# A hybrid retention and latent-attention layer on one core: the feed-forward products in a block form with seven products for eight

## The chip, the cores and the metric

The kernel is one program for one core of a Trainium2 chip. It is written in Bass: each engine has its own instruction list, and lists meet only through semaphores that the program names. The metric is the device time of one execution in microseconds (us), lower is better.

## The reference

One layer for 1024 prompt frames and 64 sample frames (1088 columns in all), model width 1024, feed-forward width 2816, everything in float32:

```python
xn = rms_norm(x, norm_mix_w)
rq, rk, rv, rg, cq, ckv, kpe, ga, gb = split_columns(xn @ w_in)
...
ret_y, mla_y, new_state = mixer_core(rq, rk, rv, q, ckv, kpe, w_ukv)
ret_branch = (head_group_norm(ret_y, ret_gn_w).astype(x.dtype) * jax.nn.silu(rg)) @ w_ret_o
mla_branch = mla_y @ w_mla_o
merged = jax.nn.sigmoid(ga) * ret_branch + jax.nn.sigmoid(gb) * mla_branch
h = x + merged @ w_out
g, u = jnp.split(rms_norm(h, norm_ffn_w) @ w_gate_up, 2, axis=-1)
h = h + (jax.nn.silu(g) * u) @ w_down
```

The final RMS norm of h is the output y. The change lies in the last two lines, the feed-forward stage.

## The kernel before

Activations lie feature-major: 128 features on the partitions, a tile for each 128 features, 1088 token columns. Each product is made of three matmuls in a reduced-precision float32 form, so that the sum has nearly float32's precision (`product`, L542 to L546): a number is split into a high part (a copy that rounds, on ScalarE) and a low part (number minus high part, on VectorE or GpSimd), and high x high, low x high and high x low are accumulated in PSUM. Weights and activations are both split.

Weights come as items: one item is the 8 blocks of 128x128 for one output tile, 512 KB. SyncE loads item n into one of two staging buffers, ScalarE writes `w_hi` (`split_high`, L848 to L855), VectorE writes `w_lo` (`split_low`, L1164 to L1169), TensorE runs the item in three column groups of 384, 384 and 320 (`item_units`, L555): 8 x 3 matmuls for each group. Six PSUM banks serve two items in turn.

The stages before the change's place are the input projection, latent attention, retention, the gated merges (two loops of items) and the output projection (`I_OUT`, 8 items), whose evacuation on VectorE (L1505) adds x and leaves h in `res`, while ScalarE squares it and VectorE sums the squares. TensorE adds these over the partitions with a matmul against ones (`feature_sums`, L583 to L591), ScalarE takes the root (`roots`, L873), VectorE the reciprocal (`inverses`, L1193), and then VectorE multiplies each tile of h by gain and reciprocal (L1207), ScalarE writes `xn_hi` (L1116), and VectorE and GpSimd take turns at `xn_lo` (L1180, L1577). TensorE's first item follows tile by tile (`streamed_item`).

The feed-forward stage (TensorE L822 to L843) goes over three groups of hidden tiles, `FFN_GROUPS` = (0, 8), (8, 8), (16, 6). For each hidden tile of a group one gate item and one up item run over the 8 tiles of xn; ScalarE applies Silu to the gate banks, VectorE multiplies with the up banks (L1534), ScalarE and VectorE split the result into `y_hi` and `y_lo`. After a group's up tiles come 8 down items over that group's tiles, and VectorE adds each to `res` (L1552). In the last group ScalarE also squares the result (L1102) and VectorE sums it (L1494) for the final norm, which ends the kernel: sums, roots, reciprocals, eight multiplies, eight stores.

All engine lists are in order: an instruction that waits holds up everything behind it on its engine.

Of the kernel before, what the change touches and what calls it, by code (L numbers as in the profile page):

```python
# [11 lines left out]
P = 128  # L28
# [17 lines left out]
FFN_GROUPS = ((0, 8), (8, 8), (16, 6))  # L46
# [97 lines left out]
def build(nc, a, o):  # L144

    with ExitStack() as ctx:
# [92 lines left out]
        res_sq = region("res_sq", 22, [TOK])  # L239
        res_inv = region("res_inv", 23, [TOK])  # L240
        norm_f = [region(f"norm_f{b}", 18 + b, [TOK]) for b in range(2)]
# [7 lines left out]
        yr_spill = nc.dram_tensor("yr_spill", (8, P, TOK), F32, kind="Internal").ap()  # L249

# [69 lines left out]
        out_done = sem("out_done")  # L320

# [50 lines left out]
        F_OUT, F_FFN, A_FFN = F_M2 + 24, F_M2 + 48, A_M2 + 24  # L372
        SUM_OUT, SUM_FIN = KT + 6, KT + 6 + 24
# [26 lines left out]
        def _(sp):  # L400
# [118 lines left out]
            with sp.Fori(0, 4) as i:  # L519
                for j in range(2):  # L520
                    for g, (c0, c1) in enumerate(GROUPS):
                        k = 3 * j + g
                        sp.wait_ge(g_free, 6 * i + (F_OUT + k - 1))
                        sp.dma_start(tmp[k % 2][:, 0:c1 - c0], a["x"][:, 2 * i + j, c0:c1])\
                          .then_inc(xres_in[k % 2], 16)
                    item_in_loop(i, I_OUT + 2 + j)
            with sp.Fori(0, (N_ITEMS - I_FFN) // 2 - 1) as i:
                for j in range(2):
                    item_in_loop(i, I_FFN + 2 + j)

            for t in range(KT):
                sp.wait_ge(scaled, 2 * KT + 6 + t + 1)
                sp.dma_start(o["y"][:, t, :], res[:, t, :]).then_inc(out_done, 16)
# [7 lines left out]
        def _(pe):  # L541
            def product(out, wh, wl, xh, xl, start=True, stop=True):  # L542

                nc.tensor.matmul(out, wh, xh, start=start, stop=False)  # L544
                nc.tensor.matmul(out, wl, xh, start=False, stop=False)  # L545
                return nc.tensor.matmul(out, wh, xl, start=False, stop=stop)  # L546
# [37 lines left out]
            def feature_sums(k, src):  # L584

                for g, (c0, c1) in enumerate(GROUPS):
                    m = 3 * k + g
                    if m >= 2:
                        pe.wait_ge(root_done, m - 1)
                    nc.tensor.matmul(ps[:, 6 + m % 2, 0:c1 - c0], ones[:, :], src[:, c0:c1],  # L590
                                     start=True, stop=True).then_inc(stat_done, 1)  # L591
# [3 lines left out]
            feature_sums(0, sumsq)  # L595
            streamed_item(I_A % 2, I_A, 0, None, xa_hi, xa_lo, lambda k: wait_low(pe, k))

            def kv_sums():
                pe.wait_ge(summed, KT + 6)
                feature_sums(2, sumsq)  # L600

            for j in range(1, N_A):
# [4 lines left out]
                if j == 4:  # L607
                    pe.wait_ge(summed, KT + 4)
                    feature_sums(1, sumsq)
# [213 lines left out]
            feature_sums(3, res_sq)  # L823
            n0, free0, act0, low0 = I_FFN, F_FFN, A_FFN, 24
            for f, (_, tiles) in enumerate(FFN_GROUPS):
                pe.wait_ge(g_free, free0 - 3)
                if f == 0:

                    streamed_item(n0 % 2, n0, 0, (g_act, act0 - 2), xn_hi, xn_lo,
                                  lambda k: wait_low(pe, KT + 4 + k))  # L830
                    item_units((n0 + 1) % 2, n0 + 1, 3, (g_free, free0 - 2), xn_hi, xn_lo)
                with pe.Fori(1 if f == 0 else 0, tiles) as i:
                    item_units(n0 % 2, 2 * i + n0, 0, (g_act, 3 * i + (act0 - 2)), xn_hi, xn_lo)
                    item_units((n0 + 1) % 2, 2 * i + (n0 + 1), 3, (g_free, 3 * i + (free0 - 2)), xn_hi, xn_lo)
                n0, free0, act0, low0 = n0 + 2 * tiles, free0 + 3 * tiles, act0 + 3 * tiles, low0 + 3 * tiles
                pe.wait_ge(g_low, low0)
                with pe.Fori(0, 4) as i:
                    for j in range(2):
                        item_units((n0 + j) % 2, 2 * i + (n0 + j), 3 * j,
                                   (g_free, 6 * i + (free0 + 3 * j - 5)), y_hi, y_lo, blocks=tiles)  # L840
                n0, free0 = n0 + 8, free0 + 24
            pe.wait_ge(summed, SUM_FIN + 24)
            feature_sums(4, res_sq)  # L843
# [3 lines left out]
        def _(act):  # L847
# [25 lines left out]
            def roots(k, width):  # L873
                for g, (c0, c1) in enumerate(GROUPS):
# [231 lines left out]
            with act.Fori(0, 4) as i:  # L1106
                for j in range(2):
                    for g, (c0, c1) in enumerate(GROUPS):
                        if g == 0:
                            act.wait_ge(g_done, 6 * i + (G_OUT + 3 * j + 1))  # L1110
                            in_loop(i, I_OUT + 1 + j)
                        residual_squares(i, j, g, c0, c1, F_OUT, SUM_OUT)
            roots(3, D_MODEL)
            for t in range(KT):
                act.wait_ge(scaled, KT + 6 + t + 1)
                nc.scalar.activation(xn_hi[:, t, :], norm_f[t % 2][:, :], ACT.Copy).then_inc(norm_high, 1)  # L1116
# [646 lines left out]
```

## Time and profile before

| what | value |
|---|---|
| time, median of 3 runs | 2310.66 us (2310.51 to 2312.24) |
| span of the profiled execution | 2308.3 us |
| TensorE matmul busy | 2131.0 us (92%) |
| VectorE, ScalarE, GpSimd busy | 912.8, 577.7, 117.4 us |
| mean granted TensorE clock | 0.963 of full |
| instructions | 32790 |

The span is the time from the first to the last instruction of the profiled execution; the time of a run is a little longer. Busy time is summed over an engine's instructions. A matmul's shown duration is longer than its distance from the next one, since matmuls overlap: to price one, read the distance between starts. The granted clock is in tenths of the full 2.4 GHz; 0.5 is the lower of its two levels, 1.2 GHz.

### The profile page before, as it was taken

To read this page: it belongs to the slowest core of one execution; us is meant where nothing else is said; L and a number is where in the kernel's file an instruction comes from. 1 tells how busy PE (TensorE), PEld (TensorE's weight loads), DVE (VectorE), ACT (ScalarE), POOL (GpSimd) and SP (SyncE) were. 2 spreads that over 40 slices of the span, in tenths; PEclk is the share of its full clock that TensorE was granted. 3 is DMA by queue.
4 is the path that set the end of the run, shared out by engine and by line. 5 is a ranking of instruction groups with operands and counts; after the bars stand their busy time and mean duration, and the time that the engine had idled before them with its cause. 6 is when DMAs were issued, how large, how long until landed. Compare 5 with 4: busy or idle time off the path is not lost.

```text
span 2308.3 us, 32790 instructions
## 1 busy us (share of the span) xinstructions
PE 2131.0 (92%) x12842; PEld 2046.4 (89%) x12842; DVE 912.8 (40%) x1620; ACT 577.7 (25%) x1069; POOL 117.4 (5%) x145
## 2 busy tenths in 40 slices
PE   3979898997989889999999999699999999999996
PEld 3957787886989879999999999699999999999995
DVE  7476767764434433311112243622222222222245
ACT  4234444441121233311211122222210211112222
POOL 2010000001112210000000000100000000000000
PEclk8989999998999999999999999799999999999998
DMA  6211111115111113211141113111111111111112
GB/s 273 63 52 33 45 44 34 39 34 216 44 45 47 57 34 89 81 46 45 45 191 45 45 46 92 40 46 45 45 46 37 46 45 45 46 44 40 44 55 86
DMA packets 62782, 144.06 MB, mean 62 GB/s; under 512 B 9713, under 2 KB 34225, under 8 KB 62705
## 3 DMA queue, kind: packets, MB, share of 16 engines
q1 hardware_dynamic: 62704, 143.00, 19.1%
q8 instruction: 52, 0.85, 0.1%
q14 instruction: 26, 0.20, 0.0%
HBM read 113.80 MB, written 29.18 MB: 62 GB/s over the span
## 4 chain that ended last, share of the span: by engine, by line
PE 79%; DVE 13%; ACT 3%; DMA 2%; issue 1%; SPq 1%; POOL 1%; DVEq 0%; ACTq 0%
PE ps L544 25%; PE ps L546 25%; PE ps L545 25%; DVE tmp L1215 1%; DVE pt_lo L1180 1%; DVE negmax L1382 1%; DVE inv L1198 1%; DVE w_lo L1168 1%; PE ps L779 1%; DMA y_lo<-ym_spill 1%; PE ps L720 1%; DVE p_exp L1390 1%; DVE norm_f L1207 1%; DMA xn_lo<-xn_spill 1%; PE ps L783 1%
## 5 line engine op out<-in xcount | busy, mean ns | idle before, releaser
L544 PE MATMUL ps<-xn_hi,w_hi 128*128 128x384 f32 (+1 forms) x2016 | 669.0, 332 | 37.7 <-DMA xn_lo<-xn_spill 12.4
L546 PE MATMUL ps<-xn_lo,w_hi 128*128 128x384 f32 (+1 forms) x2016 | 664.9, 330 | 0.0
L545 PE MATMUL ps<-xn_hi,w_lo 128*128 128x384 f32 (+1 forms) x2016 | 664.9, 330 | 0.0
L544 PEld LDWEIGHTS ps<-xn_hi,w_hi 128*128 128x128 f32 x2016 | 384.5, 191 | 44.9 <-issue 19.4
L545 PEld LDWEIGHTS ps<-xn_hi,w_lo 128*128 128x128 f32 x2016 | 384.8, 191 | 0.0
L546 PEld LDWEIGHTS ps<-xn_lo,w_hi 128*128 128x128 f32 x2016 | 384.5, 191 | 0.0
L544 PE MATMUL ps<-y_hi,w_hi 128*128 128x384 f32 (+1 forms) x912 | 299.3, 328 | 9.8 <-DVE y_lo L1180 6.3
L546 PE MATMUL ps<-y_lo,w_hi 128*128 128x384 f32 (+1 forms) x912 | 299.2, 328 | 0.0
L545 PE MATMUL ps<-y_hi,w_lo 128*128 128x384 f32 (+1 forms) x912 | 298.8, 328 | 0.0
L1168 DVE TENSOR_TENSOR w_lo<-w_stage,w_hi 128x1024 fp32r<-128x1024 f32 (+1 forms) x151 | 182.0, 1205 | 240.8 <-ACT w_hi L854 240.4
L854 ACT ACTIVATE w_hi<-w_stage 128x1024 fp32r<-128x1024 f32 (+1 forms) x151 | 156.3, 1035 | 448.0 <-PE ps L546 440.1
L544 PEld LDWEIGHTS ps<-y_hi,w_hi 128*128 128x128 f32 x912 | 172.4, 189 | 11.2 <-issue 7.1
L545 PEld LDWEIGHTS ps<-y_hi,w_lo 128*128 128x128 f32 x912 | 172.4, 189 | 0.0
L546 PEld LDWEIGHTS ps<-y_lo,w_hi 128*128 128x128 f32 x912 | 172.3, 189 | 0.0
L1534 DVE TENSOR_TENSOR tmp<-ps,tmp 128x384 f32<-128x384 f32 (+1 forms) x66 | 35.4, 536 | 250.4 <-PE ps L546 250.4
L1552 DVE TENSOR_TENSOR res<-res,ps 128x384 f32 (+3 forms) x72 | 38.3, 532 | 164.1 <-PE ps L546 164.1
L544 PE MATMUL ps<-w_hi,xn_hi 128*128 128x256 f32 (+1 forms) x288 | 84.9, 295 | 8.2 <-DVE w_lo L1168 8.2
L1002 ACT ACTIVATE p_exp<-ps,negmax 64x320 f32<-64x320 f32 (+8 forms) x72 | 51.6, 717 | 161.4 <-DVE negmax L1383 161.3
L546 PE MATMUL ps<-w_lo,xn_hi 128*128 128x256 f32 (+1 forms) x288 | 82.6, 287 | 0.0
L545 PE MATMUL ps<-w_hi,xn_lo 128*128 128x256 f32 (+1 forms) x288 | 82.6, 287 | 0.0
L544 PE MATMUL ps<-xa_hi,w_hi 128*128 128x384 f32 (+3 forms) x168 | 58.2, 346 | 18.3 <-POOL xa_lo L1577 16.3
L1124 ACT ACTIVATE tmp<-ps 128x384 f32<-128x384 f32 (+1 forms) x66 | 31.1, 473 | 171.5 <-PE ps L546 171.4
(156 smaller groups left out, 2761.7 us busy)
## 6 DMA issues: line engine op xcount, KB each, us to landing
w_stage<-in_weights SPq DMA_DIRECT2D x151, 512.0 KB, 3.6
ym_spill<-out_hl SPq DMA_DIRECT2D x32, 256.0 KB, 2.5
xt<-in_x SPq DMA_DIRECT2D x8, 544.0 KB, 6.9
xn_spill<-xa_hi SPq DMA_DIRECT2D x8, 544.0 KB, 3.6
xn_spill<-xa_lo SPq DMA_DIRECT2D x8, 544.0 KB, 4.6
xn_hi<-xn_spill SPq DMA_DIRECT2D x8, 544.0 KB, 12.1
xn_lo<-xn_spill SPq DMA_DIRECT2D x8, 544.0 KB, 13.8
y_hi<-ym_spill SPq DMA_DIRECT2D x8, 544.0 KB, 9.7
```

The source lines that it names most:

```text
L544: nc.tensor.matmul(out, wh, xh, start=start, stop=False)
L545: nc.tensor.matmul(out, wl, xh, start=False, stop=False)
L546: return nc.tensor.matmul(out, wh, xl, start=False, stop=stop)
L720: last = nc.tensor.transpose(ps[0:w, 4 + t % 2, k * P:k * P + nq], p_exp[n % 2][0:nq, (k0 + k) * P:(k0 + k) * P + w], eye[0:nq, 0:nq])
L779: nc.tensor.matmul(out, rq[b][:, c0:c1], state[:, :], start=True, stop=False)
L783: nc.tensor.matmul(ps[:, 4, 0:DV], kd_f[n % 2][0:L, :], rv[b][0:L, c, :], start=True, stop=True).then_inc(u_done, 1)
L854: nc.scalar.activation(w_hi[:, slot, first:8, :], stage[slot][:, first:8, :], ACT.Copy).then_inc(w_high, 1)
L1002: nc.scalar.activation(p_exp[n % 2][0:nq, 0:nk], src, ACT.Exp, bias=negmax[0:nq, n % 2, 0:1], scale=SCALE, accum_out=rowsum[0:nq, n % 2, 0 ...
L1124: nc.scalar.activation(tmp[g][:, 0:c1 - c0], ps[:, g, 0:c1 - c0], ACT.Silu).then_inc(g_act, 1)
L1168: nc.vector.tensor_tensor(w_lo[:, slot, first:8, :], stage[slot][:, first:8, :], w_hi[:, slot, first:8, :].bitcast(F32), ALU.subtract).the ...
L1534: nc.vector.tensor_tensor(tmp[3 + g % 2][:, 0:w], ps[:, 3 + g, 0:w], tmp[g][:, 0:w], ALU.mult).then_inc(g_free, 1)
L1552: nc.vector.tensor_tensor(res[:, 2 * i + j, c0:c1], res[:, 2 * i + j, c0:c1], ps[:, k, 0:c1 - c0], ALU.add).then_inc(g_free, 1)
```

## The change

The feed-forward stage is rewritten; everything up to the output projection stays. A product of a 2x2 block matrix of weights with a 2x2 block matrix of activations is made with seven block products and fifteen block sums (Winograd's form of Strassen's algorithm) in place of eight block products.

- **Blocks.** The activations' two block rows are the two halves of the tiles that are summed over (k), their two block columns the two halves of the tokens (544 each). The weights' two block rows are two output tiles: gate and up tile of one hidden tile in the up stage, two neighbouring output tiles in the down stage. Two items make a *pair*; there are 22 up pairs and 16 down pairs.
- **Order.** All 22 up pairs run first. The hidden result y goes to DRAM (`y_spill`) and comes back in four sets, `FFN_GROUPS` = (0, 4), (4, 6), (10, 6), (16, 6), each followed by four down pairs. m is the number of blocks in a block product: 4 in an up pair, 2, 3, 3, 3 in the sets' down pairs. Residual h is stored to DRAM (`h_spill`) during the output projection, normalised in place in `res`, and loaded again for the down stage.
- **Weights.** The seven left operands are T0 and T1 (raw blocks), T2, T3, T4, T5, T6 (raw or summed). GpSimd makes four block sums of m x 128 elements a pair (`weight_sums`), ScalarE writes high parts in four steps A to D, VectorE low parts in four steps. There is one buffer for each; a step may start when TensorE has finished with it in the pair before.
- **Activations.** The seven right operands are kept split for a whole stage (`sx_hi`, `sx_lo`) or set (`sy_hi`, `sy_lo`, one buffer each). For x, VectorE makes three sums and GpSimd one; VectorE splits operands 0, 3, 2, 4 and GpSimd 1, 5, 6 (low parts). For each set of y, GpSimd makes all four sums (S1 to S4) and the low parts of 5 and 6; VectorE splits 0, 1, 3, 4, 2 in that order. Each of these instructions has m x 544 elements (S1, S2 and operand 3 in m pieces).
- **TensorE.** The seven products go to bank pairs X, Y, X, Z, X, Z, X; each has two column groups of 272. Where a bank pair is used again within a pair, the partial sum is first copied out (ScalarE in the up stage; VectorE adds it to `res` in the down stage) while the next matmuls accumulate onto what stands in the bank.
- The code of the stage is unrolled; the loops of before are gone.

TensorE's list, whole:

```diff
+            def seven_products(pair):
+                m, s = pair_blocks(pair), set_of(pair)
+                high, low = (sx_hi, sx_lo) if s == 0 else (sy_hi, sy_lo)
+                for j, name in enumerate("XYXZXZX"):
+
+                    pe.wait_ge(tw_low, 4 * pair + (1, 1, 2, 3, 4, 3, 4)[j])
+                    if pair == 0 or opens_set(pair):
+                        operand_ready(s, j)
+
+                    if j == X_OPENS and pair >= 2:
+                        pe.wait_ge(x_full, pair - 1)
+                    elif j == Y_OPENS and pair:
+                        pe.wait_ge(y_full, pair)
+                    elif j == Z_OPENS and pair:
+                        pe.wait_ge(z_full, pair)
+                    elif j in (2, 4, 5, 6):
+                        pe.wait_ge(x_part, 4 * pair + {2: 1, 4: 2, 5: 3, 6: 4}[j])
...
+                    for half in range(2):
+                        cols = slice(QUARTER * half, QUARTER * (half + 1))
+                        for k in range(m):
...
+                            last = product(out[:, half, :], wh, wl, high[j][:, k, cols], low[j][:, k, cols],
...
+                    last.then_inc(q_done, 1)
```

VectorE at the entry of the stage:

```diff
+            weights_low(0, "A")
             inverses(3, res_inv)
...
+            normalised(0)
+            normalised(1)
+            for k in range(2):
+                dve.wait_ge(s_high, k + 1)
+                low(sx_lo[0][:, 2 * k:2 * k + 2, :], quadrant(0)[:, 2 * k:2 * k + 2, :],
+                    sx_hi[0][:, 2 * k:2 * k + 2, :]).then_inc(s_low_v, 1)
+            normalised(2)
+            normalised(3)
+            weights_low(0, "B")
...
+            nc.vector.tensor_tensor(s1_x[:, :, :], quadrant(2), quadrant(3), ALU.add).then_inc(s_sum_v, 1)
...
+            nc.vector.tensor_tensor(quadrant(2), quadrant(0), quadrant(2), ALU.subtract).then_inc(s_sum_v, 1)
...
+            nc.vector.tensor_tensor(quadrant(0), s1_x[:, :, :], quadrant(0), ALU.subtract).then_inc(s_sum_v, 1)
...
+            low(sx_lo[3][:, :, :], s1_x[:, :, :], sx_hi[3][:, :, :]).then_inc(s_low_v, 1)
...
+            low(sx_lo[2][:, :, :], quadrant(0), sx_hi[2][:, :, :]).then_inc(s_low_v, 1)
+            weights_low(0, "C")
...
+            low(sx_lo[4][:, :, :], quadrant(2), sx_hi[4][:, :, :]).then_inc(s_low_v, 1)
+            weights_low(0, "D")
```

VectorE and GpSimd in a down pair (`s` is set in the last pair of a set, `n` is the next pair, `more` says that there is one):

```diff
+                dve.wait_ge(q_done, 7 * pair + 1)
+                accumulate(lower, 0, "X").then_inc(x_part, 1)
...
+                accumulate(lower, 0, "Y").then_inc(y_full, 1)
+                if more:
+                    weights_low(n, "A")
+                dve.wait_ge(q_done, 7 * pair + 3)
+                accumulate(upper, 0, "X").then_inc(x_part, 1)
+                if more:
+                    weights_low(n, "B")
+                if s:
+                    operand_low(s, 0)
+                dve.wait_ge(q_done, 7 * pair + 4)
+                accumulate(upper, 1, "Z").then_inc(x_part, 1)
+                if s:
+                    operand_low(s, 1)
...
+                accumulate(upper, 1, "X").then_inc(x_part, 1)
+                if s:
+                    operand_low(s, 3)
...
+                accumulate(upper, 0, "Z").then_inc(z_full, 1)
+                if more:
+                    weights_low(n, "C")
+                if s:
+                    operand_low(s, 4)
...
+                accumulate(lower, 1, "X").then_inc(x_full, 1)
+                if more:
+                    weights_low(n, "D")
+                if s:
+                    operand_low(s, 2)
...
+                if more:
+                    weight_sums(n, 0)
+                if s:
+                    first_sums(s)
+                if more:
+                    weight_sums(n, 1)
...
+                if s:
+                    other_sums(s)
```

## Rows read from the trace of the kernel before

**Rows 1.** The page: two engines' totals, and the granted clock in 40 slices.

```profile
PE 2131.0 (92%) x12842; PEld 2046.4 (89%) x12842; DVE 912.8 (40%) x1620; ACT 577.7 (25%) x1069; POOL 117.4 (5%) x145
PEclk8989999998999999999999999799999999999998
```

**Rows 2.** Busy time by stretch: us, PE, PEld, DVE, ACT, POOL, PEclk, DMA share, GB/s.

```profile
1461.30:1503.70 42.40, 23.11 (x78) 19.11 (x78) 31.51 (x18) 15.76 (x18) 10.02 (x4) 0.68 0.00 1
1503.70:2283.50 779.80, 773.46 (x4680) 772.45 (x4680) 200.25 (x293) 148.41 (x225) 0.00 (x0) 1.00 0.15 44
```

**Rows 3.** Chain that ended last, 1461 to 1476 us: start, us, engine, tile, line.

```profile
1461.44 0.50 DVE res L1505
...
1464.47 0.59 ACT tmp L879
1465.09 6.99 DVE res_inv L1198 x3
1472.10 1.36 DVE norm_f L1207
1473.49 1.12 ACT xn_hi L1116
```

**Rows 4.** Who waited for whom, TensorE, 1461 to 2300 us: total, times, longest.

```profile
PE ps L544 <- DVE y_lo L1180: 6.3, 3, 2.1
```

**Rows 5.** Timeline of TensorE: 384, 320 and 256 columns; start, us, engine, line.

```profile
1600.79 0.33 PE L544 MATMUL ps<-xn_hi,w_hi 128*128 128x384 f32 x1
...
1601.31 0.33 PE L544 MATMUL ps<-xn_hi,w_hi 128*128 128x384 f32 x1
...
1679.94 0.31 PE L544 MATMUL ps<-xn_hi,w_hi 128*128 128x320 f32 x1
...
1680.38 0.31 PE L544 MATMUL ps<-xn_hi,w_hi 128*128 128x320 f32 x1
...
591.23 0.28 PE L544 MATMUL ps<-w_hi,xn_hi 128*128 128x256 f32 x1
...
591.59 0.28 PE L544 MATMUL ps<-w_hi,xn_hi 128*128 128x256 f32 x1
```

**Rows 6.** Instruction groups by shape: busy us, mean ns of one, idle before.

```profile
L1168 DVE TENSOR_TENSOR w_lo<-w_stage,w_hi 128x1024 fp32r<-128x1024 f32 x143 | 176.5, 1234 | 237.7 <-ACT w_hi L854 237.3
L1180 DVE TENSOR_TENSOR xn_lo<-norm_f,xn_hi 128x1088 fp32r<-128x1088 f32 x4 | 5.2, 1288 | 1.2 <-ACT xn_hi L1116 1.2
L1577 POOL TENSOR_TENSOR xn_lo<-norm_f,xn_hi 128x1088 fp32r<-128x1088 f32 x4 | 10.0, 2505 | 613.8 <-ACT xn_hi L1116 613.8
L1585 POOL TENSOR_TENSOR tmp<-tmp,tmp 128x384 f32<-128x384 f32 x8 | 8.1, 1010 | 106.4 <-DVE tmp L1215 106.4
L854 ACT ACTIVATE w_hi<-w_stage 128x1024 fp32r<-128x1024 f32 x143 | 151.3, 1058 | 448.0 <-PE ps L546 440.1 <-DMA w_stage<-in_weights 7.9
L1124 ACT ACT_TABLE_LOAD x8 | 10.3, 1283 | 25.0 <-PE ps L546 25.0
```

**Rows 7.** Timeline of VectorE and GpSimd where they meet, in four stretches.

```profile
618.18 1.23 DVE L1168 TENSOR_TENSOR w_lo<-w_stage,w_hi 128x1024 fp32r<-128x1024 f32 x1
618.23 2.05 POOL L1585 TENSOR_TENSOR rq<-tmp,tmp 128x384 f32<-128x384 f32 x1 [5.08 <-DVE tmp L1215]
...
552.17 1.02 POOL L1585 TENSOR_TENSOR rq<-tmp,tmp 128x384 f32<-128x384 f32 x1 [32.95 <-DVE tmp L1215]
552.33 1.94 DVE L1168 TENSOR_TENSOR w_lo<-w_stage,w_hi 128x1024 fp32r<-128x1024 f32 x1 [0.25 <-ACT w_hi L854]
...
1479.77 2.51 POOL L1577 TENSOR_TENSOR xn_lo<-norm_f,xn_hi 128x1088 fp32r<-128x1088 f32 x1 [2.61 <-ACT xn_hi L1116]
1479.78 4.91 DVE L1207 SCALAR_TENSOR_TENSOR norm_f<-res,gains,res_inv 128x1088 f32<-128x1088 f32 x2
...
627.28 0.42 DVE L1434 SCALAR_TENSOR_TENSOR s_prompt<-s_prompt,ps 128x256 f32<-128x256 f32 x1
627.33 0.88 POOL L1585 TENSOR_TENSOR rq<-tmp,tmp 128x320 f32<-128x320 f32 x1 [2.29 <-DVE tmp L1215]
```

**Rows 8.** The page, DMA issues: count, KB each, median us from issue to landing.

```profile
w_stage<-in_weights SPq DMA_DIRECT2D x151, 512.0 KB, 3.6
```

**Rows 9.** Timeline of TensorE after an idle stretch in the entry.

```profile
1477.30 0.66 PE L544 MATMUL ps<-xn_hi,w_hi 128*128 128x384 f32 x1 [10.52 <-POOL xn_lo L1577]
...
1480.76 0.34 PE L546 MATMUL ps<-xn_lo,w_hi 128*128 128x384 f32 x1
```

**Rows 10.** Chain that ended last, 2283.5 us to the end.

```profile
2284.59 0.50 DVE res_sq L1494
```

More of the change, by code:

```diff
@@ L371, in build, with down_of, pair_item @@
         F_M2, A_M2 = F_M1 + 24, A_M1 + 24
-        F_OUT, F_FFN, A_FFN = F_M2 + 24, F_M2 + 48, A_M2 + 24
-        SUM_OUT, SUM_FIN = KT + 6, KT + 6 + 24
+        F_OUT, F_FFN = F_M2 + 24, F_M2 + 48
+        SUM_OUT = KT + 6
+        SC_FFN = KT + 6
+        SC_FIN = SC_FFN + 16
+        group_items = [I_FFN + sum(2 * c + 8 for _, c in FFN_GROUPS[:f]) for f in range(len(FFN_GROUPS))]
+        def down_of(pair):
+            group, i = divmod(pair - UP_PAIRS, 4)
+            return group, 3 - i
+        def pair_item(pair):
+            if pair < UP_PAIRS:
+                f = max(f for f, (first, _) in enumerate(FFN_GROUPS) if first <= pair)
+                return group_items[f] + 2 * (pair - FFN_GROUPS[f][0])
+            f, p = down_of(pair)
+            return group_items[f] + 2 * FFN_GROUPS[f][1] + 2 * p
@@ L533, in _ @@
+            for t in range(KT):
+                sp.wait_ge(scaled, SC_FIN + t + 1)
                 sp.dma_start(o["y"][:, t, :], res[:, t, :]).then_inc(out_done, 16)
@@ L1152, in _, with out_tile @@
-            roots(4, D_MODEL)
+            def out_tile(i, j, split):
+                for g, (c0, c1) in enumerate(GROUPS):
+                    if g == 0 and split:
+                        act.wait_ge(g_done, 6 * i + (G_OUT + 3 * j + 1))
+                        in_loop(i, I_OUT + 1 + j)
+                    residual_squares(i, j, g, c0, c1, F_OUT, SUM_OUT)
+            with act.Fori(0, 3) as i:
+                for j in range(2):
+                    out_tile(i, j, True)
+            out_tile(3, 0, True)
@@ L1566, in _, with out_tile @@
[L1566 to L1568 removed]
+            def out_tile(i, j, split):
+                for g, (c0, c1) in enumerate(GROUPS):
+                    k = 3 * j + g
+                    w = c1 - c0
+                    dve.wait_ge(g_done, 6 * i + (G_OUT + k + 1))
+                    dve.wait_ge(xres_in[k % 2], 48 * i + 16 * (k // 2 + 1))
+                    nc.vector.tensor_tensor(res[:, 2 * i + j, c0:c1], ps[:, k, 0:w], tmp[k % 2][:, 0:w],
+                                            ALU.add).then_inc(g_free, 1)
+                    if g == 0 and split:
+                        in_loop(i, I_OUT + 1 + j)
+                    residual_sum(i, j, g, c0, c1, SUM_OUT)
```

672 lines of the change are left out of this document (516 added, 156 removed).

## The prediction

> **What bounds the kernel now.** I read the granted clock and the engine totals first: TensorE works for 92% of the span, VectorE for 40%, GpSimd for 5% [rows 1]. Then I read the busy times by stretch. The feed-forward stage runs from the last product of the output projection (1461.3 us) to its own last product (2283.5 us), so 822.2 us. In 779.8 us of it TensorE is busy for 773.5 us at full clock; the other three engines have room [rows 2]. So what counts is how many columns TensorE streams, plus the places where it waits. There are two kinds of these: the entry, 42.4 us in which only 78 TensorE instructions start, bound by reciprocals and by VectorE and GpSimd work in turn [rows 2, 3], and three waits of 2.1 us where an up group turns into a down group [rows 4].
>
> **Products.** Starts lie 0.520 us apart for three 384-column products (173.5 ns each), 0.440 for three of 320 (146.7) and 0.360 for three of 256 (120) [rows 5]. That is a line: 0.417 ns a column and 13 ns beside. Before: (22 x 2 x 8 + 8 x 22) x 3 x 3 = 4752 products of 384, 384 and 320 columns, 164.6 ns on average. The window gives 773.46 us / 4680 = 165.3 ns [rows 2], which is 1.004 of that. After: an up pair has 7 products x 2 halves x 4 blocks x 3 = 168 of 272 columns; 22 of them make 3696. A down pair has 42 x m with m = 2, 3, 3, 3, four pairs each: 1848. Together 5544. For 272 columns the line gives 126.7 ns, with 1.004 127.3; the bounds are the two nearest rows, 120 and 146.7 ns. Sum 5544 x 127.3 = **705.7 us** against 4752 x 165.3 = 785.5: a gain of 79.8 us, less than an eighth because each product has 13 ns beside its columns. One block product takes 3.04 us in an up pair (21.3 us for seven), 1.52 for m = 2 (10.6), 2.28 for m = 3 (16.0).
>
> **Prices of the side work.** VectorE, two operands in SBUF: 1088 elements 1.29 us, 1024 1.23, 384 0.56. GpSimd: 1088 2.50, 384 1.01, so 544 1.35, 512 1.28, 1632 3.65, 2176 4.8. ScalarE: 1088 1.11, 1024 1.06 [rows 6]; 1632 by the same slope 1.57. The scaled multiply takes 1.35 us for 1088 [rows 3].
>
> **VectorE and GpSimd take turns.** A GpSimd sum of 384 takes 1.02 us alone and 2.05 us when a VectorE w_lo (1.23 us) has just started; a w_lo behind such a sum takes 1.94; two VectorE multiplies that meet a 2.51 us GpSimd instruction take 4.91 in place of 2.6. A VectorE instruction that reads PSUM beside one SBUF operand is not delayed (0.42 us at 627.28 beside GpSimd's 0.88) [rows 7]. So I charge every VectorE instruction with two SBUF operands and every GpSimd instruction to one shared line, one after the other. The Trainium skill, "Advanced Engine Details and Errata", section VectorE Performance Modes, names only VectorE's 2p instructions as those that block GPSIMD, and its table gives tensor_tensor no 2p mode; by that section alone nothing here would be charged twice, which is the first rival. The trace disagrees with it for these forms [rows 7].
>
> **Steady pairs: nothing to pay.** In an up pair the shared line carries 4 x 1.28 + 1.35 (GpSimd) and 3 x 1.23 + 0.69 + 2 x 0.72 (VectorE) = 12.3 us of 21.3. ScalarE has four splits and six PSUM passes, about 7.6. Walking through the waits in order, each thing that TensorE asks for is there over 2 us early (tightest: the p5 copy, which starts when product 3 ends and is wanted by product 5, and D's split at 3 us for product 4 at 12.2). If that cover went, each us lost in a pair would cost 22. The down pairs carry 5.5 to 9 us of 10.6 or 16. On SP's queue the residual spills stand between the loads of x in the output projection, and a pair's two loads ahead of the y spills; the DMA share is 0.15 [rows 2] and 512 KB land in 3.6 us [rows 8], each wanted over 15 us after its issue. I cost them at zero; uncovered, one would cost its landing, about 4 us.
>
> I number products and operands 0 to 6 as the code does; splits A to D are the steps of the weights (T0 and T1; T2; T3 and T5; T6 and T4).
>
> **Entry.** Time from 1461.3. The residual add, last square, last sum and split A end at 4.4 us; the reciprocals take 6.98 -> 11.4. From here the shared line never rests. Normalising quadrants 0 and 1 (5.9) and two half splits of operand 0 (2.6) -> 19.9: product 0 starts. GpSimd splits operand 1 (4.8) -> 24.7. Quadrants 2 and 3 (5.9), split B (0.7), three sums (7.3) -> 38.6. Split of operand 3 (2.4), GpSimd's difference (4.8), split of operand 2 (2.4) -> 48.3: only now product 2. GpSimd splits 5 (4.8), split C (1.2), GpSimd splits 6 (4.8), split of 4 (2.4), split D (1.3) -> 62.8, which product 4 waits for. VectorE's first evacuation (c11) stands behind D in its queue, the Silu waits for it and, with a table load of 1.28 us [rows 6], holds up ScalarE's next copy (u2), which product 4 also waits for: 66.1. Products 4 to 6 end at 75.2, some 2.5 us go to the clock, so pair 0 ends at 77.7, **56.4 us** more than its own 21.3. Before, the entry costs 42.4 - 72 x 0.165 = 30.5.
>
> **Up to down (pairs 21 and 22, m = 2).** From GpSimd's sum at 15.9 us of pair 21 the shared line carries u3 + p5 1.35, S1 2.7, S3 2.5, S2 2.7, S4 2.5 and the splits of 5 and 6 2.5 each = 16.8 (GpSimd), and C, D, y, y and the splits of operands 0, 1, 3, 4, 2 = 9.5 (VectorE) -> 42.1. Operand 2 is last in VectorE's list and wanted third by TensorE. A weight sum of GpSimd slips in and the evacuation of product 0 follows in VectorE's queue, so product 2 starts at 43.6 and pair 22 ends at 51.2 where 31.9 would do: **19.3 us**.
>
> **Set to set (three times).** Take a last pair with m = 3 before another with m = 3; time from its first product. GpSimd: first weight sums 1.9 -> 3.9; S1 (4.05) and S3 (3.65), with VectorE's split A between, -> 12.6; only then the third and fourth weight sums -> 14.6. ScalarE's split B waits for the third (13.6), and behind it in its queue stand the splits of operands 1 and 3. VectorE: split B -> 15.2, split of operand 0 -> 17.0, then the evacuation of product 3 -> 17.8, without which product 5 doesn't start; TensorE wants it at 11.4. Its last product ends at 23.4 in place of 16. The line goes on with S2, S4, splits 5, 6 and VectorE's splits of 1, 3, C, 4, D, 2: in all 26.7 (GpSimd: 4 x 1.01, 2 x 4.05, 4 x 3.65) and 13.0 (VectorE) us after 1.9, with 1 us of rest, -> 42.6. The evacuation of product 0 stands behind it (0.75): product 2 of the new set starts at 43.4, its pair ends at 54.8 where 31.9 would do: **22.9 us**. After the m = 2 set, with 10.6 us of products as cover, 54.5 against 26.6: **27.9**. With up to down: 19.3 + 27.9 + 2 x 22.9 = 93.0. Before, a change of group costs 2.1 us, three times [rows 4].
>
> **Clock.** After 10.5 us of idleness TensorE ran at 1.2 GHz for 3.46 us, eleven products that need 1.8 at 2.4 GHz [rows 9]: 1.65 us lost. Four changes of set with 12 to 17 us of idleness: 6.8. **Tail:** the last square and sum are 544 wide and the sum moves from VectorE to GpSimd (0.50 to 1.35 us) [rows 6, 10]: +1.5.
>
> **Sum.** After: 705.7 + 56.4 + 93.0 + 6.8 = 861.9, against 822.2: +39.7, tail +1.5, so +41.2. The span 2308.3 becomes 2349.5; the median stands 2.4 above the span: **2352 us**.
>
> **Rivals.**
> - *Side by side* (faster). If VectorE and GpSimd did not hold each other up, the same walk gives 34.7 for the entry (VectorE free at 44.2), 5.2 for up to down, 13.5 + 2 x 8.5 for the sets, 2 for the clock: 705.7 + 72.4 = 778.1, so 822.2 - 778.1 - 1.5 = 42.6 us gained: 2268. The break-even is where half of the 84 us of turns is really paid. For: on the page VectorE is idle for 60% and GpSimd for 95% of the span [rows 1]; against: every meeting in [rows 7]. Chance 0.12.
> - *VectorE first.* If VectorE always won the turn, its list would end near 35 instead of 42.6 and each change would lose some 8 us less, the entry 10: about 2311. Against: the waits in [rows 7] go both ways. Chance 0.10, spread over 2295 to 2325.
> - *Slow restarts.* If TensorE stayed at 1.2 GHz for whole pairs after the idle stretches, the three changes and the entry would each lose 5 to 8 us more: 2375 to 2390. The trace's longest slow stretch after an idle one in this stage is the one of [rows 9]. Chance 0.06.
> - *No seven for eight.* If a 272-column product took what a 320-column one does, 5544 x 19.4 ns = 108 us more: 2460. Against: 256 columns do go at 120 ns [rows 5]. Chance 0.02.
> - My forecast, 2325 to 2375: 0.70.
>
> Two in ten are left out by 2300 to 2378. A measurement of this kernel tells 0.2% (4.6 us) from no change. Faster: the first rival and a third of the second, 0.16; same 0.03; slower 0.81.
>
> **What would show it.** Right: 12,842 + 792 = 13,634 TensorE instructions, starts of 272-column ones 127 ns apart; up pairs 21.3 us apart with no wait; TensorE waiting 12 to 17 us for VectorE's split of operand 2 at four places; GpSimd instructions of 1632 elements near 3.7 us alone, and VectorE's w and y splits at two or three times their own time beside them. Wrong: idle TensorE under 6 us at the set changes (turns don't add up), up pairs over 22 us (the cover is gone), or product starts off 127 ns.

## The result and the profile after

The changed kernel takes **2330.21 us** (median of four, 2327.66 to 2333.38) against 2310.59 (four) before: ratio 1.008, interval 1.0066 to 1.0095. It is slower, as forecast, but by 19.6 us and not by 41. The profiled execution has a span of 2331.6 us. Of the page, the engine totals and the granted clock:

```profile
PE 2060.2 (88%) x13636; PEld 1974.1 (85%) x13636; DVE 1123.6 (48%) x1715; ACT 686.9 (29%) x1174; POOL 465.4 (20%) x375
...
PEclk9989999998999899999999999799999999878988
```

TensorE has 13,636 instructions (13,634 forecast) and is busy for 2060 us where it was busy for 92% of 2308 [rows 1]. GpSimd went from 5% to 20%. The clock now dips in the down stage too. Busy time by stretch (us, then PE, PEld, DVE, ACT, POOL, PEclk, DMA share, GB/s): the entry with pair 0, the up pairs 1 to 21 without any stop, and the down pairs:

```profile
1465.95:1539.40 73.45, 29.64 (x175) 27.63 (x176) 65.23 (x39) 27.54 (x26) 35.01 (x13) 0.72 0.11 37
1539.40:1981.50 442.10, 442.10 (x3530) 441.90 (x3528) 161.18 (x169) 155.86 (x212) 138.68 (x108) 1.00 0.23 83
1984.40:2306.20 321.80, 251.12 (x1848) 248.34 (x1848) 214.88 (x200) 87.17 (x106) 180.47 (x112) 0.87 0.22 77
```

The stage runs from the end of the output projection (1465.95) to its last product (2306.19): **840.2 us**, against 822.2 before [rows 2]. The middle row gives 442.10 / 3530 = 125.2 ns a product, at full clock: the side work is hidden, as costed. TensorE's waits from 1500 us on (total, times, longest):

```profile
PE ps L741 <- DVE res L1965: 70.6, 8, 14.1
PE ps L741 <- ACT p L1394: 19.6, 1, 19.6
PE ps L741 <- ACT u L1394: 6.7, 1, 6.7
```

The first row is the four changes of set, where before there were three waits of 2.1 us [rows 4]. Four of its eight waits are at product 2 of a new set (10.5, 14.1, 11.7 and 11.9 us, where 12 to 17 were forecast), the others at products 4 and 5 of the pair before one. L1965 is VectorE's evacuation, which in its queue stands behind the splits. The two rows of ScalarE (L1394) are waits at the entry, at products 2 and 4. The change from the second to the third set, pairs 29 and 30, which begin at 2116.7 and 2141.8 (start, us, engine, line, tiles; in brackets the idle time before):

```profile
2118.92 1.02 POOL L2084 TENSOR_TENSOR raw_w<-raw_w 128x384 f32<-128x384 f32 x1 [9.24 <-DVE t_lo L1521]
2120.02 1.01 POOL L2086 TENSOR_TENSOR raw_w<-raw_w 128x384 f32<-128x384 f32 x1
2120.99 4.72 POOL L2122 TENSOR_TENSOR s_y<-raw_y 128x544 f32<-128x544 f32 x3
2125.78 3.67 POOL L2125 TENSOR_TENSOR raw_y<-raw_y 128x1632 f32<-128x1632 f32 x1
2129.53 0.99 POOL L2091 TENSOR_TENSOR raw_w<-raw_w 128x384 f32<-128x384 f32 x1
...
2133.87 6.07 POOL L2133 TENSOR_TENSOR raw_y<-s_y,raw_y 128x544 f32<-128x544 f32 x3 [2.26 <-DVE sy_lo L1521]
2140.08 4.02 POOL L2138 TENSOR_TENSOR raw_y<-raw_y 128x1632 f32<-128x1632 f32 x1
2145.95 8.93 POOL L2099 TENSOR_TENSOR sy_lo<-raw_y,sy_hi 128x1632 fp32r<-128x1632 f32 x2 [1.85 <-ACT sy_hi L1410]
```

```profile
2131.94 1.84 DVE L1521 TENSOR_TENSOR sy_lo<-raw_y,sy_hi 128x1632 fp32r<-128x1632 f32 x1
...
2137.47 7.21 DVE L1521 TENSOR_TENSOR sy_lo<-s_y,sy_hi 128x544 fp32r<-128x544 f32 x3
...
2146.11 5.29 DVE L1521 TENSOR_TENSOR sy_lo<-raw_y,sy_hi 128x1632 fp32r<-128x1632 f32 x1
...
2151.95 3.74 DVE L1521 TENSOR_TENSOR t_lo<-raw_w,t_hi 128x768 fp32r<-128x768 f32 x1
2155.62 1.84 DVE L1521 TENSOR_TENSOR sy_lo<-raw_y,sy_hi 128x1632 fp32r<-128x1632 f32 x1
2157.39 1.53 DVE L1965 TENSOR_TENSOR res<-res,ps 128x544 f32<-128x544 f32 x2
```

```profile
2158.24 0.57 PE L741 MATMUL ps<-sy_hi,t_hi 128*128 128x272 f32 x1 [11.71 <-DVE res L1965]
2158.61 0.43 PE L742 MATMUL ps<-sy_hi,t_lo 128*128 128x272 f32 x1
2158.83 0.43 PE L743 MATMUL ps<-sy_lo,t_hi 128*128 128x272 f32 x1
2159.06 0.43 PE L741 MATMUL ps<-sy_hi,t_hi 128*128 128x272 f32 x1
```

These rows show the turns. A VectorE split of 1632 elements takes 1.84 us alone (2131.94) and 5.29 beside GpSimd's (2146.11), and GpSimd's S2 (L2133) takes 6.07 where S1 (L2122) took 4.72. The third weight sum (L2091) waits behind S1 and S3, as the walk had it. VectorE's split of operand 2 (2155.62) is the last one, and the evacuation of product 0 (2157.39) stands behind it. So product 2 of the new set starts at 2158.24 after 11.7 us of idleness, and its first products are 0.23 us apart, at the lower clock.

From the timelines of TensorE I take for every kernel what is lost beside the products. At the entry it is the end of pair 0 after the end of the output projection, less 21.05 us. At a change it is the length of the two pairs less what they take in steady state (21.05, 10.52, 15.82 us); in the last four kernels the change from set 3 to 4 also has 1.7 us that are lost one pair later. The last row is the forecast, its 6.8 us of clock spread over the four changes.

| kernel | entry | up to down | set 1-2 | 2-3 | 3-4 | sum | span |
|---|---|---|---|---|---|---|---|
| changed kernel | 52.4 | 18.1 | 27.7 | 22.5 | 23.8 | 144.5 | 2331.6 |
| GpSimd fills only | 39.5 | 11.4 | 18.7 | 15.4 | 12.8 | 97.8 | 2281.4 |
| weight sums first | 52.4 | 18.1 | 27.3 | 22.9 | 24.0 | 144.7 | 2327.0 |
| S1, S3 a pair earlier | 52.3 | 18.1 | 23.6 | 18.0 | 16.7 | 128.7 | 2313.0 |
| y sets on VectorE | 52.3 | 13.6 | 14.0 | 7.7 | 9.2 | 96.8 | 2279.1 |
| entry too | 45.6 | 13.5 | 14.0 | 7.7 | 9.2 | 90.0 | 2271.6 |
| and copies first | 35.5 | 13.4 | 13.9 | 7.6 | 9.2 | 79.6 | 2261.8 |
| and order tidied | 35.5 | 9.1 | 11.6 | 5.2 | 6.8 | 68.2 | 2251.8 |
| forecast | 56.4 | 21.0 | 29.6 | 24.6 | 24.6 | 156.2 | 2349.5 |

In each the stage is 5544 x 125.3 = 694.7 us, plus the sum, plus about 1.1. With 822.2 us before, the block form breaks even at a sum of some 126 us. Spans also differ by where the output projection ends, 1460.5 to 1466.0 us, in stages that none of these kernels changed; the changed kernel's profiled execution has the latest, 4.65 us behind the one of before.

### The profile page after: what moved, and what is told of

It is laid out like the page before. It is cut to its first block, busy times and chain, and to the rows that moved or that the text cites. A ratio compares the mean times of both kernels' runs of the same rounds, so it can differ in the third digit from the quotient of the medians.

```text
span 2331.6 us, 33876 instructions
## 1 busy us (share of the span) xinstructions
PE 2060.2 (88%) x13636; PEld 1974.1 (85%) x13636; DVE 1123.6 (48%) x1715; ACT 686.9 (29%) x1174; POOL 465.4 (20%) x375
## 4 chain that ended last, share of the span: by engine, by line
PE 72%; DVE 18%; ACT 3%; issue 2%; POOL 2%; DMA 2%; SPq 1%; DVEq 0%; ACTq 0%; POOLq 0%
PE ps L741 23%; PE ps L742 22%; PE ps L743 22%; DVE sy_lo L1521 3%; DVE t_lo L1521 1%; DVE tmp L1556 1%; DVE pt_lo L1521 1%; DVE negmax L1723 1%; DVE inv L1539 1%; DVE w_lo L1509 1%; DVE sx_lo L1521 1%; PE ps L976 1%; DMA y_lo<-ym_spill 1%; DVE p_exp L1731 1%; PE ps L980 1%
## 5 line engine op out<-in xcount | busy, mean ns | idle before, releaser
L741 PE MATMUL ps<-sx_hi,t_hi 128*128 128x272 f32 x1232 | 355.6, 289 | 41.4 <-ACT p L1394 19.6
L743 PE MATMUL ps<-sx_lo,t_hi 128*128 128x272 f32 x1232 | 358.3, 291 | 0.0
L742 PE MATMUL ps<-sx_hi,t_lo 128*128 128x272 f32 x1232 | 357.5, 290 | 0.0
L741 PE MATMUL ps<-xn_hi,w_hi 128*128 128x384 f32 (+1 forms) x960 | 321.4, 335 | 20.5 <-DMA xn_lo<-xn_spill 12.6
L743 PE MATMUL ps<-xn_lo,w_hi 128*128 128x384 f32 (+1 forms) x960 | 318.2, 331 | 0.0
L742 PE MATMUL ps<-xn_hi,w_lo 128*128 128x384 f32 (+1 forms) x960 | 318.1, 331 | 0.0
L741 PEld LDWEIGHTS ps<-sx_hi,t_hi 128*128 128x128 f32 x1232 | 235.0, 191 | 42.6 <-issue 41.6
L741 PE MATMUL ps<-sy_hi,t_hi 128*128 128x272 f32 x616 | 186.5, 303 | 73.6 <-DVE res L1965 70.6
L743 PEld LDWEIGHTS ps<-sx_lo,t_hi 128*128 128x128 f32 x1232 | 234.1, 190 | 0.0
L742 PEld LDWEIGHTS ps<-sx_hi,t_lo 128*128 128x128 f32 x1232 | 233.9, 190 | 0.0
L741 PEld LDWEIGHTS ps<-xn_hi,w_hi 128*128 128x128 f32 x960 | 184.5, 192 | 24.6 <-DMA xn_lo<-xn_spill 15.8
L741 PEld LDWEIGHTS ps<-sy_hi,t_hi 128*128 128x128 f32 x616 | 123.7, 201 | 76.3 <-issue 75.0
L743 PEld LDWEIGHTS ps<-xn_lo,w_hi 128*128 128x128 f32 x960 | 184.2, 192 | 0.0
```

Of the source, the lines that this page charges most:

```text
L741: nc.tensor.matmul(out, wh, xh, start=start, stop=False, skip_group_check=onto)
L742: nc.tensor.matmul(out, wl, xh, start=False, stop=False, skip_group_check=onto)
L743: return nc.tensor.matmul(out, wh, xl, start=False, stop=stop, skip_group_check=onto)
```

## The experiments

**The turns taken away.** GpSimd's instructions in the stage become fills that read nothing; VectorE, ScalarE and TensorE are untouched, and the results are left out with the sums. `fill_only` is two whole fills and one of a fifth of the tile; the edit is the same for every sum, difference and split.

```diff
-                    nc.gpsimd.tensor_tensor(b12, b12, b11, ALU.subtract).then_inc(tw_sum, 1)
+                    fill_only(b12).then_inc(tw_sum, 1)
```

> The changed kernel with each of GpSimd's sums, differences and splits in the feed-forward stage replaced by fills of the same tile that read nothing (two whole fills and one of a fifth, one after the other), so that GpSimd is busy about as long and at the same places of its queue and everything still waits for it as before. It leaves out what those instructions compute. Theory (the turns are paid: VectorE's instructions with two SBUF operands and GpSimd's that read SBUF exclude each other): fills don't take part, so the stalls fall to those of the first rival of the prediction, entry about 31, up to down about 5, sets about 13 and twice 8, some 70 in place of 144.5 us; the span about 2258 us (2245 to 2275), VectorE's 2176-element splits of the entry at 2.4 us each. Rival (GpSimd is just slow and in the wrong order, VectorE is not held up by it): the stalls stay within 10 us of 144.5, span 2322 to 2342.

One run, 2283.2 us: 46.7 us of stalls are gone, not 74. The groups of VectorE by shape in pairs 29 and 30 (busy us, mean ns of one, idle before), first of the changed kernel, then of this one, and GpSimd's fills of the splits of operands 5 and 6:

```profile
L1521 DVE TENSOR_TENSOR sy_lo<-raw_y,sy_hi 128x1632 fp32r<-128x1632 f32 x4 | 11.6, 2890 | 0.0
L1521 DVE TENSOR_TENSOR t_lo<-raw_w,t_hi 128x768 fp32r<-128x768 f32 x6 | 10.1, 1690 | 0.7 <-ACT t_hi L1365 0.7
```

```profile
L1522 DVE TENSOR_TENSOR sy_lo<-raw_y,sy_hi 128x1632 fp32r<-128x1632 f32 x4 | 7.4, 1854 | 0.5 <-ACT sy_hi L1411 0.5
L1522 DVE TENSOR_TENSOR t_lo<-raw_w,t_hi 128x768 fp32r<-128x768 f32 x6 | 5.7, 956 | 0.9 <-ACT t_hi L1366 0.9
```

```profile
2112.45 2.98 POOL L2019 MEMSET sy_lo<- 128x1632 f32 x2 [3.88 <-ACT sy_hi L1411]
2115.48 0.37 POOL L2021 MEMSET sy_lo<- 128x324 f32 x1
```

GpSimd is busy for 3.40 us per operand in place of 3.65 alone, and VectorE no longer loses anything beside it. So the exclusion is between VectorE's two SBUF inputs and GpSimd's reads, since the fills still write, and it costs up to 46.7 us (a part of that is the fills being 0.25 us shorter, an estimated 1 us for each change to a set of m = 3). It isn't all: 97.8 us stay, 39.5 at the entry and 58.3 at the changes of set. The third weight sum still stands behind S1 and S3 (product 5 of pair 29 starts at 17.0 us, not 11.3). In the new set's first pair the next pair's third weight sum stands behind GpSimd's fills for operands 5 and 6, and behind that sum come split B and the evacuation that product 5 needs: product 5 starts 5.6 us after product 4, not 2.3, while VectorE itself rests for 5.6 us. What holds TensorE there is the order of GpSimd's queue. The Trainium skill, "SBUF — State Buffer", section "SBUF: two separate sides", calls the shared port pair "an exclusive lock, not a bandwidth split", taken by a VectorE instruction with two SBUF inputs only against a GpSimd instruction that reads SBUF. The two traces agree with both halves: 2890 against 1854 ns.

**The order in GpSimd's queue.**

```diff
-                if s:
-                    first_sums(s)
                 if more:
                     weight_sums(n, 1)
+                if s:
+                    first_sums(s)
```

> The changed kernel with one thing moved: in the last pair before a new set GpSimd makes the third and fourth weight sums before S1 and S3, not behind them. Theory (what counts is the total of one shared line of VectorE and GpSimd): product 5 of that pair no longer waits (pair 25, 29 and 33 end some 6 to 7 us earlier), but product 2 of the new set starts at the same time within 2 us, and the span is 2331 within 4 us. Rival (GpSimd's order in its queue causes the loss: B and with it VectorE's queue stand behind S1 and S3): each of three changes gets 6 to 9 us shorter, span 2304 to 2313.

One run, 2328.8 us. Pair 29 ends after 18.2 us in place of 25.2, and product 2 of the next pair starts at 23.7 in place of 16.4: 41.9 against 41.6 us from the start of pair 29. The three changes give 27.3, 22.9, 24.0 us against 27.7, 22.5, 23.8. What is won at product 5 is paid at product 2, as the shared line has it; the rival's 6 to 9 us a change are not there. TensorE's wait has only moved (total, times, longest; the changed kernel had 70.6, 8, 14.1):

```profile
PE ps L741 <- DVE res L1965: 74.5, 9, 19.0
```

**Work taken off the line's busy stretch.**

```diff
-                if s:
-                    first_sums(s)
                 if more:
                     weight_sums(n, 1)
+                if more and p == 1 and set_of(pair) < len(FFN_GROUPS):
+                    first_sums(set_of(pair) + 1)
```

> The changed kernel with S1 and S3 of the second, third and fourth set of the down stage made one pair earlier (their raw data has long landed), behind that pair's weight sums. Theory (one line): 7.7 us of GpSimd work for m = 3 leave the line's busiest stretch and go where the line has 7 us of rest (pairs of 15.8 us with 9 us of work, of 10.5 us with 5.5 to 9), so each of the changes to sets of m = 3 gets 6 to 9 us shorter, 18 to 27 us in all: span 2304 to 2313, still as long as the kernel before within 5 us; product 5 of the last pair no longer waits. Rival (product 2 waits for something else than the line's total, a DMA or ScalarE's queue): under 8 us in all, over 2323.

Ten runs, median 2313.7 us, ratio to before 1.0013 (1.0003 to 1.0023). The changes got 4.1, 4.5 and 7.1 us shorter, 15.7 in all: direction and place right, size below the 18 to 27 expected. S1 and S3 were 8.4 us of the line (4.72 and 3.67). In pair 29, which begins at 2109.8 here, GpSimd's S2 now starts 11.1 us after the first product and not 17.2, so 6.1 of the 8.4 came back, and product 2 of the next pair comes 6.1 us earlier (35.5 and not 41.6). GpSimd's first three weight sums of the pair:

```profile
2113.31 1.01 POOL L2084 TENSOR_TENSOR raw_w<-raw_w 128x384 f32<-128x384 f32 x1 [2.48 <-DVE t_lo L1521]
2114.40 1.02 POOL L2086 TENSOR_TENSOR raw_w<-raw_w 128x384 f32<-128x384 f32 x1
2116.47 1.02 POOL L2091 TENSOR_TENSOR raw_w<-raw_w 128x384 f32<-128x384 f32 x1 [1.05 <-DVE t_lo L1521]
```

The first starts 3.5 us into the pair and not 2.2: it waits for VectorE's splits of the pair before, which the moved S3 now delays (split C takes 2.99 us beside it). Before the third GpSimd rests for 1.05 us until VectorE's split A is done, which S1 used to cover. These two are the missing 2.3 us. Another 1.5 us are lost behind product 2. So work taken off the line is worth its length only as far as it does not meet other work where it goes, and no other wait is next.

**The disputed duration.** This is the kernel before, with TensorE's products of the stage cut to widths of 272, 304 and 256 columns in the three groups (the other columns are left out):

```diff
                 c0, c1 = GROUPS[g]
+                if narrow:
+                    c1 = c0 + narrow[g]
```

> The kernel before with TensorE's products in the feed-forward stage cut to the first 272, 304 and 256 columns of the three token groups (the other columns are left out), in its old loops. It measures the term of the sum that was off. Line of the prediction (0.417 ns a column and 13 ns): starts 126.7, 139.8 and 119.7 ns apart. Rival (a 272-column product really takes 125.3 anywhere, as in the changed kernel's steady pairs; the line is not straight): 272 at 125.3 within 0.3. If 272 comes out at 126.7 here, the form of the new loop (two halves, one stationary after the other) is what made it shorter. Span: 786 us of products become 8 x 198 x 3 x 0.1287 = 611.6, but some waits of the side work may open: 2130 to 2160 us.

Span 2137.0 us. Over whole blocks of 24 products the starts lie 119.5, 125.3 and 137.9 ns apart for 256, 272 and 304 columns. Starts of 272-column products in the old loop (the first column), and busy time by stretch:

```profile
1559.92 0.29 PE L544 MATMUL ps<-xn_hi,w_hi 128*128 128x272 f32 x1
1560.05 0.29 PE L545 MATMUL ps<-xn_hi,w_lo 128*128 128x272 f32 x1
...
1561.43 0.28 PE L544 MATMUL ps<-xn_hi,w_hi 128*128 128x272 f32 x1
```

```profile
1560.00:2000.00 440.00, 435.81 (x3402) 435.41 (x3401) 133.18 (x191) 97.51 (x145) 0.00 (x0) 1.00 0.18 57
```

1561.43 - 1559.92 is 12 products, 126 ns with the rounding of the column. So 272 columns cost 125.3 ns in either loop, as the rival had it and not 126.7; the straight line through 256, 320 and 384 was wrong between its points. By steps: 0.36 ns a column from 256 to 272, 0.39 from there to 304, 0.55 to 320 (146.7), 0.42 to 384 (173.5).

**The y sets on VectorE.** On a line where both exclude each other, the engine that needs half the time should do the work: S2, S4 and the splits of operands 5 and 6 go to VectorE. The run also makes S1 and S3 a pair earlier and splits in TensorE's order, in part inside a set's first pair, so it does not price the choice of engine alone (`o` is set in the first pair of the second to fourth set):

```diff
-        S_LOW_V_N = {0: 1, 1: 2, 3: 3, 4: 4, 2: 5}
-        S_LOW_P_N = {5: 1, 6: 2}
+        S_LOW_V_N = {j: j + 1 for j in range(7)}
...
+                if o:
+                    operand_low(o, 3)
...
+                if o:
+                    fourth_sum(o)
+                    operand_low(o, 4)
```

> The changed kernel with the arithmetic of the four y sets moved: S2, S4 and the splits of operands 5 and 6 go from GpSimd to VectorE (1.86 us for 1632 elements in place of 3.65), S1 and S3 stay on GpSimd but one pair earlier, the operands are split in the order in which TensorE takes them, and operands 3 to 6 of a set are split inside its first pair. The entry is untouched. Theory (one shared line, and what it has to carry before a product starts): per change to an m = 3 set the line then carries 7 x 1.86 for the splits, 2 x 1.86 for S2 and S4, two pairs of weight splits 7.0 and GpSimd's weight sums 8, with VectorE's 13 sums from PSUM 9.4 beside them, 45 us, of which some 35 stand before the last operand is ready 27 us later: 8 to 11 us of stall in place of 22.5 to 27.7; up to down 2 to 5 in place of 18.1. In all 92 becomes 30 to 40: span 2270 to 2282, faster than the kernel before by 1.2 to 1.7%. Rival (from the run with fills: half of the stalls stay where nothing takes turns, so GpSimd's pace isn't what counts but that the work must lie in these two pairs): 20 us less at most, over 2300.

Four runs, 2280.9 us, ratio 0.9874 (0.9859 to 0.9889), now faster than before. The set changes fell to 14.0, 7.7, 9.2 us (8 to 11 expected), but up to down only to 13.6, where 2 to 5 were expected; that is 44.5 us for the four, above the 30 to 40 expected, with a span of 2279.1 inside the 2270 to 2282. At up to down product 0 of pair 22 is done long before VectorE evacuates it, since the evacuation stands behind D and the splits of operands 4 to 6 in VectorE's queue. That is the longest wait here, 9.3 us:

```profile
PE ps L741 <- DVE res L1991: 29.8, 11, 9.3
```

**The entry too.** GpSimd's splits of operands 1, 5 and 6 of x and its difference go to VectorE, in the order in which TensorE takes them; ScalarE's first copy and VectorE's first evacuation move ahead of later splits.

```diff
-            operand_low(0, 1, quadrant(1))
+            first_low(1, quadrant(1))
```

> The same, and at the entry too GpSimd keeps only the weight sums: VectorE splits all seven operands of x and makes the fourth sum, in the order in which TensorE takes them, and its first evacuation stands ahead of the last splits. Theory (one line): the walk gives, from the end of the output projection, reciprocals to 11.4, four normalised quadrants 11.8, seven splits 17 and four sums 9.7 at 2.42 us, weight splits 1.8 and small waits, so product 2 starts at 41 in place of 46.6, the last split is ready at 52.5 and pair 0 ends at 57 to 60 in place of 73.5: 13 to 16 us less than the run without this part. Rival (GpSimd's splits ran beside work that had to be waited for anyway): under 5 us less, as VectorE now carries it all.

Five runs, 2274.6 us, ratio 0.9846 (0.9833 to 0.986). Product 2 starts at 39.6 us after the output projection (41 expected; 46.7 in the changed kernel), but pair 0 ends at 66.7 and not at 57 to 60: the entry lost 6.7 us, not the 13 to 16 expected. The rows of GpSimd and ScalarE show what the walk had left out:

```profile
1507.66 6.78 POOL L2139 TENSOR_TENSOR raw_w<-raw_w 128x512 f32<-128x512 f32 x1 [40.60 <-DVE t_lo L1532]
1514.52 1.26 POOL L2141 TENSOR_TENSOR raw_w<-raw_w 128x512 f32<-128x512 f32 x1
1515.92 1.26 POOL L2146 TENSOR_TENSOR raw_w<-raw_w 128x512 f32<-128x512 f32 x1
```

```profile
1517.21 0.63 ACT L1365 ACTIVATE t_hi<-raw_w 128x512 fp32r<-128x512 f32 x1 [9.45 <-POOL raw_w L2146]
1517.75 0.60 ACT L1382 ACTIVATE p<-ps 128x544 f32<-128x544 f32 x1
```

A weight sum of 1.26 us takes 6.78 beside three VectorE instructions in a row, and two more follow; ScalarE's split B of pair 1 waits for them, and the copy p5, which product 5 needs and which was due at about 1508, stands behind it.

**The copies first.**

```diff
-                weights_high(n, "B")
+                if pair:
+                    weights_high(n, "B")
...
                 part(u3, pair, "X").then_inc(x_part, 1)
+                if pair == 0:
+                    weights_high(n, "B")
```

> The run with everything on VectorE, with one step of pair 0 moved: on ScalarE the copies of products 3 and 4 (p5, u3) stand before the split B of pair 1, not behind it. In the run before, product 5 of pair 0 started at 41.6 us of the pair where 34 would do: the copy p5 stood behind split B, B behind GpSimd's third weight sum, and that behind the first, which took 6.78 us beside VectorE's splits of operands 5 and 6 in a row. Theory (that chain, and nothing else, is what the entry lacked against its walk): product 5 starts near 34, product 6 near 37.5, pair 0 ends at 56.5 to 58 us after the output projection in place of 66.7, 8 to 10 us less: 2265 us. Rival (TensorE's last two products wait for the splits of operands 5 and 6 themselves, or for the slow clock): under 3 us less.

Four runs, 2263.4 us, ratio 0.9797 (0.9782 to 0.9812). Product 5 starts at 34.1 us of the pair in place of 41.6, product 6 at 37.1, pair 0 ends at 56.5, all within 0.4 us of what was expected or inside its range; the sum falls by 10.4 us (8 to 10 expected). So the chain was the one that held pair 0. The copy p5 now starts when its product is done:

```profile
1508.49 0.62 ACT L1382 ACTIVATE p<-ps 128x544 f32<-128x544 f32 x1 [0.17 <-PE ps L743]
```

**The order tidied.** Operands are split in another order, split D of a set's first pair goes behind that pair's first evacuation, and the first set is now treated like the others (`o` is set in its first pair too).

```diff
-        S_HIGH_N = {j: j + 1 for j in range(7)}
+        S_HIGH_N = {0: 1, 1: 2, 3: 3, 2: 4, 4: 5, 6: 6, 5: 7}
...
                 accumulate(lower, 0, "X").then_inc(x_part, 1)
                 if o:
-                    operand_low(o, 3)
+                    operand_low(o, 4)
+                    weights_low(pair, "D")
```

> The same with the order of the set changes tidied: operand 3 is split before operand 2, split D of a set's first pair goes from the end of the pair before to behind that pair's first evacuation, and the up to down change is treated like the others (its operands 4 to 6 are split inside the first down pair, whose first evacuation so stands before them). The work on the shared line is the same. Theory: up to down loses 13.6 us because the first evacuation stands behind D and the splits of operands 4 to 6; with these behind it 5 to 8 us are left; at the three other changes only VectorE's 2 us of rest are used: 1 to 2 us each. In all 9 to 13 us less than the run without this part: 2253 to 2257 us. Rival (the line's total alone decides, whatever the order): up to down also stays within 2 us, 3 us less at most.

Five runs, **2253.6 us, ratio 0.9753** (0.974 to 0.9766): 57 us faster than the kernel before. Up to down lost 4.3 us (9.1 stay, 5 to 8 expected), the others 2.3 to 2.4 each (1 to 2 expected), 11.4 in all (9 to 13). The rival, that the line's total alone decides, had 3 us at most. The stage, and TensorE's waits by VectorE's evacuations:

```profile
1461.94:2225.88 763.94, 710.81 (x5551) 704.84 (x5550) 421.62 (x434) 273.84 (x348) 276.84 (x206) 0.98 0.24 84
```

```profile
PE ps L741 <- DVE res L2007: 17.5, 9, 5.4
```

## Why the prediction was right in direction and off in size

The direction came out, and the mechanism with it, but the loss is 19.6 us where 41.2 were forecast: what failed is the size of three terms (products, entry, changes of set), all charged too high, so that none made up for another. Forecast and profiled span differ by 2349.5 - 2331.6 = 17.9 us: the stage came out 21.7 below its 861.9, the tail 0.9 below, and 4.65 us were added by stages that the change doesn't touch. By its terms:

- **Products, the term that was mis-sized most.** 705.7 forecast, 694.7 measured: 11 us, half of the gap in the stage. The step that failed is "for 272 columns the line gives 126.7 ns, with 1.004 127.3". The product costs 125.3, in the old loop too; over 5544 products 2.0 ns is 11 us. Of the 2.0 ns the straight line is 1.4. The factor 1.004, the excess over the starts in the window of before, is the rest (126.7 x 1.004 is 127.2, so 0.1 of it is rounding): the window of after, 125.2 ns a product, shows no such excess. The bounds beside it, 120 and 146.7, held.
- **Steady pairs.** Costed at zero, and so it is: pairs 1 to 20 are all 21.05 us, with no wait.
- **Entry.** 56.4 forecast, 52.4 measured. The walk has the right order of waits, but for one: product 2 waited not for the split of operand 2 alone (done at 1512.19) but for ScalarE's copy of product 0 (done at 1512.48), which stood behind the split of operand 5 in ScalarE's queue. Here that cost 0.3 us; the same kind of wait came back in the run with the entry on VectorE. Split D ended at 60.1 us, not 62.8, and from there to product 4 it took 2.0 us, not 3.3: the table load of 1.28 us lay before the Silu at 1513.4, in ScalarE's idle time, and was not on the path.
- **Changes of set.** 93.0 forecast and 6.8 for the clock, 92.1 measured for both, 7.7 less. Product 5 of pair 29 started at 17.9 us (17.8 forecast), product 2 of the new set at 41.6 (43.4); at the other changes it came 1.9 to 2.9 us before the walk as well. So the line was charged about 5% too much, and all of that behind the start of S2 (17.2 us in pair 29, where the walk has 17.0). One part can be read from the rows: a VectorE instruction behind another starts some 0.08 us before the recorded end of the one before (in the run with fills a split of 1.85 us at 2101.43, the next at 2103.20), and the walk added whole durations. Over some ten of them that is an estimated 0.8 of the 1.8 us in this change. The rest isn't settled.
- **Clock.** There are 194 products at about 226 ns in the stage, nearly all in twelve stretches of 10 to 25 products after a wait, 19.5 us in all, where the forecast counted 9.3. Most stand ahead of a further wait, which covers them; at the four changes 1.3 to 2.6 us between product 2 and the end of the pair are not covered, which is near the 1.65 assumed.
- **The rivals.** "Side by side" was refused by the rows before, and the run with fills shows what it would have been: 97.8 us of stalls, not the 72 of its walk. The walk without turns was thus too kind by 25 us. It let the order of the queues off lightly, as the rests in the run with fills show; how the 25 us divide over its steps was not worked out. "Slow restarts" for whole pairs don't occur: the longest slow stretch has 25 products of a pair's 126. "VectorE first" is refused by turns lost on both sides (6.07 on GpSimd, 5.29 on VectorE). "No seven for eight" falls with 125.3 ns.

The deeper question, why an eighth fewer products makes the kernel slower, is answered by the table: the form gains 785.5 + 6 - 694.7, some 97 us, and pays 114 more in stalls (144.5 against 30.5 at the entry before, the three waits of 2.1 being in the 6). Of these, 46.7 go when the two engines no longer exclude each other, and 76.3 in the last kernel, which keeps every operation of the change but has most of the y and x work on VectorE, early and in TensorE's order. By steps of the table, 37.6 of the 76.3 came from time and order alone (15.8 for S1 and S3 a pair earlier, 10.4 for the copies, 11.4 for the order), and 38.7 from the two runs that moved work to VectorE and changed its time and order as well. What the engine alone is worth was not measured. The block form pays; its first placement didn't.

## What to carry to other kernels

Where VectorE and GpSimd instructions both read two operands from SBUF, count them on one line. Giving the work of a busy stretch to VectorE, which needs half the time, is the argument behind the largest step here (31.9 us), though no run changed the engine alone. Ask of every evacuation what stands before it in its engine's queue: a copy of 0.6 us behind a split that waited for a starved weight sum cost 10 us, and reordering cost nothing. A duration between two measured sizes is a measurement to make, not a point on a line, when it is multiplied by thousands.

## What the hardware showed that was not expected

- Products in the reduced-precision float32 form (fp32r in the rows) start 119.5, 125.3, 137.9, 146.7 and 173.5 ns apart for 256, 272, 304, 320 and 384 columns: 0.36 to 0.55 ns a column, in steps that a line doesn't fit.
- GpSimd's fills don't disturb a VectorE instruction with two SBUF inputs (1854 ns for 1632 elements beside them, 2890 beside sums).
- A GpSimd instruction that meets several such VectorE instructions in a row can wait for all of them: 6.78 us for one of 1.26, beside two splits of 2.4 and one of 1.2 us.
- The activation table for the Silu was loaded while ScalarE waited for the Silu's input in the changed kernel, and cost nothing; in the run with the entry on VectorE ScalarE had no idle time there and the load stood on its queue's path.
